# Gate tiles and turned q and k by two products, of 512 and of 256 columns, with their halves added by GpSimd, in place of three products of 256

## The reference, cut to what matters

```
# block 1
(q_a, k_a, v_a, f_a, q_b, k_b, v_b, q_c, c_kv, q_i, k_i, w_i, gates) = jnp.split(h @ w_in, ...)
...                                   # forgetting, stick-breaking and top-k attention
g_a, g_b, g_c = jnp.split(jax.nn.sigmoid(gates), N_BRANCH, axis=-1)
merged = (g_a * (y_a @ w_up_fox) + g_b * (y_b @ w_up_sb) + g_c * (y_c @ w_up_dsa))
return merged @ w_out
# block 2
q_a, k_a, v_a, q_b, k_b, v_b, gate_a, gate_b = jnp.split(h @ w_in, IN_OFFSETS, axis=-1)
...                                   # windowed attention and block attention
mixed = jax.nn.sigmoid(gate_a) * y_a + jax.nn.sigmoid(gate_b) * y_b
x = x + gt1[:, None, :] * (mixed @ w_out)
```

## Time and profile before

| | us |
|---|---|
| median of 3 runs | 2033.84 |
| lowest, highest | 2031.59, 2033.9 |
| the profiled execution | 2032.25 |
| its span | 2030.6 |
| PE busy in the span | 1960.0 (97%) |
| DVE busy | 1526.7 (75%) |
| ACT busy | 1031.0 (51%) |
| POOL busy | 44.9 (2%) |

### The profile page before, as it was taken

How to read it: one execution, slowest core, us unless ns; L and a number is a source line. 1 busy time by engine, 2 the same in 40 slices (tenths; PEclk the granted TensorE clock), 3 DMA queues, 4 the chain that set the end, 5 groups by cost and what they waited for, 6 DMA issues and landing times.

```text
span 2030.6 us, 32702 instructions
## 1 busy us (share of the span) xinstructions
PE 1960.0 (97%) x11980; PEld 1718.1 (85%) x11980; DVE 1526.7 (75%) x2637; ACT 1031.0 (51%) x1582; POOL 44.9 (2%) x80
## 2 busy tenths in 40 slices
PE   7999999999999999999899999999999999999998
PEld 6888898988888888899888888888788888887887
DVE  7887567579888987657678887785767778667766
ACT  5445545654446444545565445566444455555443
POOL 0000000000000000000000000000000000000000
PEclk9999999999999999999999999999999999999999
DMA  7874543257774876453246774441455544233553
GB/s 298 293 283 172 190 156 131 88 180 280 277 268 153 287 281 215 167 186 125 94 169 247 282 250 150 170 149 71 145 186 186 186 179 173 95 125 135 186 186 135
DMA packets 77286, 382.18 MB, mean 188 GB/s; under 512 B 9296, under 2 KB 9472, under 8 KB 55936
## 3 DMA queue, kind: packets, MB, share of 16 engines
q1 hardware_dynamic: 67392, 329.78, 44.9%
q0 software_dynamic: 9792, 51.00, 7.6%
HBM read 379.65 MB, written 1.10 MB: 188 GB/s over the span
## 4 chain that ended last, share of the span: by engine, by line
PE 82%; DVE 9%; ACT 6%; issue 3%; DMA 1%; SPq 0%; DVEq 0%; ACTq 0%
PE psum L674 21%; PE psum L585 15%; PE psum L586 15%; PE psum L587 15%; PE psum L677 11%; DVE weights_low_a L1446 2%; ACT weights_high_a L1069 1%; PE psum L883 1%; ACT x_normed L1077 1%; PE psum L821 1%; PE psum L812 1%; PE psum L910 1%; PE psum L911 1%; PE psum L909 1%; DMA raw_a<-in_w_ffn_a_a 1%
## 5 line engine op out<-in xcount | busy, mean ns | idle before, releaser
L674 PE MATMUL psum<-h_high_low,weights_high_a 128*128 128x512 f32 x1840 | 654.7, 398 | 5.4 <-DVE h_high_low L1491 3.3
L1446 DVE TENSOR_TENSOR weights_low_a<-raw_a,weights_high_a 128x2048 fp32r<-128x2048 f32 (+1 forms) x232 | 459.8, 1983 | 123.2 <-ACT weights_high_a L1069 121.2
L677 PE MATMUL psum<-h_high_low,weights_low_a 128*128 128x256 f32 x1840 | 514.2, 279 | 0.0
L674 PEld LDWEIGHTS psum<-h_high_low,weights_high_a 128*128 128x128 f32 x1840 | 345.3, 188 | 92.5 <-issue 5.3
L1069 ACT ACTIVATE weights_high_a<-raw_a 128x2048 fp32r<-128x2048 f32 (+1 forms) x232 | 386.0, 1664 | 65.1 <-PE psum L587 61.4
L677 PEld LDWEIGHTS psum<-h_high_low,weights_low_a 128*128 128x128 f32 x1840 | 346.7, 188 | 6.6 <-issue 1.0
L1446 DVE TENSOR_TENSOR weights_low_b<-raw_b,weights_high_b 128x1024 fp32r<-128x1024 f32 x224 | 273.3, 1220 | 54.5 <-ACT weights_high_b L1069 54.0
L1069 ACT ACTIVATE weights_high_b<-raw_b 128x1024 fp32r<-128x1024 f32 x224 | 235.4, 1052 | 104.6 <-PE psum L587 104.6
L1139 ACT ACTIVATE up_low_products<-psum 128x512 f32<-128x512 f32 (+1 forms) x146 | 74.1, 507 | 391.7 <-PE psum L677 391.6
L585 PE MATMUL psum<-weights_high_b,gated_high 128*128 128x512 f32 x608 | 241.8, 398 | 4.6 <-DVE gated_low L1575 2.8
L587 PE MATMUL psum<-weights_high_b,gated_low 128*128 128x512 f32 x608 | 241.3, 397 | 0.0
(11 more groups left out here) (300 smaller groups left out, 3165.9 us busy)
## 6 DMA issues: line engine op xcount, KB each, us to landing
ada_weights<-in_w_ada POOLq DMA_DIRECT2D x64, 768.0 KB, 5.9
raw_a<-in_w_ffn_a_a SPq DMA_DIRECT2D x44, 1024.0 KB, 7.3
raw_a<-in_w_ffn_b_a SPq DMA_DIRECT2D x44, 1024.0 KB, 7.4
raw_a<-in_w_ffn_a SPq DMA_DIRECT2D x64, 512.0 KB, 4.4
raw_b<-in_w_ffn_b SPq DMA_DIRECT2D x64, 512.0 KB, 3.3
raw_a<-in_w_proj_a SPq DMA_DIRECT2D x28, 1024.0 KB, 5.5
raw_a<-in_w_gate_a SPq DMA_DIRECT2D x26, 1024.0 KB, 4.8
raw_b<-in_w_ffn_a_b SPq DMA_DIRECT2D x44, 512.0 KB, 3.9
```

The source lines that it names most:

```text
L674: pe.matmul(ps[:, bank, :], whi[0][:, p, c:c + P], hboth[:, k, :, :].rearrange("p a b -> p (a b)"), start=k == 0, stop=False, skip_group_c ...
L677: last_mm = pe.matmul(ps[:, bank, SEQ:2 * SEQ], wlo[0][:, p, c:c + P], hhi[:, k, :], start=False, stop=k == KD - 1, skip_group_check=True)
L1446: dve.tensor_tensor(wlo[kind][:, p, 0:width], raw[kind][:, p, 0:width], whi[kind][:, p, 0:width].bitcast(F32), ALU.subtract).then_inc(lo_r ...
```

## The change

The two forms of product get one function, `mm2`. In each of the 832 steps, one matmul of 512 columns multiplies the high weights with `hhi` and `hlo`, and one of 256 columns adds the low weights by `hhi` to the second half. ACT copies the whole bank (512 columns) to SBUF, and GpSimd adds the second half onto the first. The second half of a copy lies where the first half of the next tile goes, so each copy waits until the add before it is done (`halves_added`). The q and k tiles and the gates of block 1 become one tensor for that, with a spare tile at its end. PE waits for the twelfth add before the first tick of block 1, and the turning of the gates waits for the adds instead of for the copies.

```
+            def mm2(both_halves, w_hi, w_lo, k, start, stop):
+
+                pe.matmul(both_halves, w_hi, hboth[:, k, :, :].rearrange("p a b -> p (a b)"), start=start, stop=False,
+                          skip_group_check=True)
+                return pe.matmul(both_halves[:, SEQ:2 * SEQ], w_lo, hhi[:, k, :], start=False, stop=stop,
+                                 skip_group_check=True)
...
@@ gate_tile (PE)
-                    m = mm3(ps[:, g % 2, 0:SEQ], hi, lo, hhi[:, k, :], hlo[:, k, :], k == 0, k == KD - 1)
+                    m = mm2(ps[:, g % 2, :], hi, lo, k, k == 0, k == KD - 1)
...
@@ project_turned (PE)
-                        m = mm3(ps[:, bank, 0:SEQ], whi[kind][:, n % 2, c:c + P], wlo[kind][:, n % 2, c:c + P],
-                                hhi[:, k, :], hlo[:, k, :], k == 0, k == KD - 1)
+                        m = mm2(ps[:, bank, :], whi[kind][:, n % 2, c:c + P], wlo[kind][:, n % 2, c:c + P],
+                                k, k == 0, k == KD - 1)
...
@@ ticks (PE)
                 pe.wait_ge(now().proj_copied, 20 if blk == 1 else 12)
+                if blk == 1:
+                    pe.wait_ge(now().halves_added, QK_TILES)
...
@@ GpSimd
+            def add_halves(tile, copied, value):
+
+                pool.wait_ge(copied, value)
+                pool.tensor_tensor(tile[:, 0, :], tile[:, 0, :], tile[:, 1, :], ALU.add).then_inc(now().halves_added, 1)
...
+                if blk == 2:
+                    for g in range(GATE2_TILES):
+                        add_halves(g2[:, g:g + 2, :], now().gate_copied, g + 1)
                 if blk == 1:
 
+                    for i in range(QK_TILES):
+                        add_halves(turned_and_gates[:, i:i + 2, :], now().proj_copied, 8 + i + 1)
+                    for g in range(GATE1_TILES):
+                        add_halves(g1[:, g:g + 2, :], now().gate_copied, g + 1)
                     pool.wait_ge(now().scale_ready, 2 * NT + 1)
                     ada_loads(l, 1)
...
@@ project_turned (ACT)
-                    copy_projection(w.mark[g], qk1[:, s, m, :], ps[:, (g + 8) % ROW_BANKS, 0:SEQ],
+                    if g:
+                        act.wait_ge(now().halves_added, g)
+                    copy_projection(w.mark[g], turned_and_gates[:, g:g + 2, :].rearrange("p a b -> p (a b)"),
+                                    ps[:, (g + 8) % ROW_BANKS, :],
                                     SCALE if s in (0, 2) else 1.0)
...
@@ gate_tile (ACT)
-                act.activation((g1 if blk == 1 else g2)[:, g, :], ps[:, g % 2, 0:SEQ],
+                added = g + (QK_TILES if blk == 1 else 0)
+                if added:
+                    act.wait_ge(now().halves_added, added)
+                act.activation((g1 if blk == 1 else g2)[:, g:g + 2, :].rearrange("p a b -> p (a b)"), ps[:, g % 2, :],
                                ACT.Copy).then_inc(now().gate_copied, 1)
...
@@ gate_tanh (ACT)
-                act.wait_ge(now().gate_copied, (f + 1) * n)
+                act.wait_ge(now().halves_added, (f + 1) * n + (QK_TILES if blk == 1 else 0))
```

More of the change, by code:

```diff
@@ L39 @@
 YT2 = 8
+QK_TILES, GATE1_TILES, GATE2_TILES = 12, 24, 16
 TA, TB = 16, 8
@@ L128, in __init__ @@
         self.gate_copied = one("gate_copied")
+        self.halves_added = one("halves_added")
         self.gates_ready = one("gates_ready")
@@ L349, in build @@
         tt2 = put("turned_two", [P, 14, SEQ])
-        g2 = put("gates_two", [P, 16, SEQ])
+        g2 = put("gates_two", [P, GATE2_TILES + 1, SEQ])
         y2 = put("y_two", [P, NT, YT2 * P])
```

5 lines of the change are left out of this document (3 added, 2 removed).

## The result

The median went from 2033.84 us to 2043.22 us (5 runs of each, 2037.06 to 2044.91 for the changed kernel). The ratio is 1.0042, with a 95% interval of 1.0031 to 1.0054: slower by 8.5 us, between 6 and 11. The forecast was 2030.5 us, and the result lies outside its range. The profiled execution of the changed kernel is the slowest of its five, 2044.91 us with a span of 2043.2.

The account below looks back on a forecast made before the run. PE was taken to bound the kernel, with 82% of the chain of waits. Products -7.2, copies +2.2 and passage +1.7 summed to -3.3 us: 2030.5 us, own range 2028 to 2033.5, over all rivals 2027.2 to 2039.5.

Parts of the forecast that it names:

- the gain of the products: Turned q and k and gates of both blocks: two matmuls a step in place of three, 7.2 us gained together.
- the passage: Turned projection to block 1's first tick: PE waits for the last add, 0.85 us longer, twice, 1.7 us.
- The step on PE: Turned and gate tiles: a step falls from 360 to 349.7 ns, 10.3 ns less, bounds 7.5 and 13.
- The weights by the chain's shares: Gates in the ticks: 74% of block 1's gain and 87% of block 2's count; turned tiles all on the path.
- The copies: ACT's copies of 512 columns: 0.22 us more each, 104 times; only those in the chain count, 2.2 us.
- The adds in the ticks: 104 GpSimd adds of 529 ns each, 55 us spread over 455 us; POOL never late, no cost in the ticks.
- rival (b): Passage and ticks: (a), and the clock falls too; 2039.5 to 2042.7, say 2041 us; chance 12%.
- (a): Passage and ticks: GpSimd and DVE hold each other up, +2.3 and +3.2 us, 2036.0 us in all; chance 30%.

Follow-up runs that it names:

- free adds of a tile to itself: The change without its own adds, plus 104 GpSimd adds of a spare tile to itself that nobody waits for; against the kernel before: 2033.62 us, 1.0005.
- free adds of two different rows: The change without its own adds, plus 104 GpSimd adds of two different constant rows, nobody waiting; against the kernel before: 2035.80 us, 1.0015.
- the spare rows: The change with PE's wait moved to the first scores and second halves copied to two spare rows in turn; against the kernel before: 2037.06 us, 1.0021.
- the fills: The kernel before plus 104 GpSimd memsets of 128x256, which write SBUF and read nothing, nobody waiting: 2033.75 us, 0.9999.
- the adds alone: The kernel before plus 104 GpSimd adds of a spare tile to itself, released by the same copies, nobody waiting: 2037.03 us, 1.0019.
- the late wait: The change with PE's wait for the twelfth add moved from before the first gate tile to the first scores reading q and k: 2038.76 us, 1.0022.

## Why the prediction was wrong

The runs form a ladder, in which each kernel has one thing more than the one above it. Each step is uncertain by about 2.6 us, the last by 3, so the four small ones don't stand clear of the noise by themselves; the two rows of free adds together (+4.2) and the last step do.

```
                                          ratio    step, us   forecast, us
products alone                            0.9987     -2.6       -7.2
+ copies of 512                           0.9994     +1.4       +2.2
+ free adds of a tile to itself           1.0005     +2.2     }   0
+ free adds of two different rows         1.0015     +2.0     }
+ copies, tanh, scores behind the adds    1.0022     +1.4         0
+ the wait before the first gate tile     1.0042     +4.1       +1.7
sum                                                  +8.5       -3.3
```

The sum is off by 11.8 us, at three steps: the gain of the products came out 4.6 us too small, adds that nobody waits for were put at nothing and take 4.2, and the passage takes 2.4 more than was put down.

- **The step on PE was nearly right.** "I take the middle, 349.7 ns: 10.3 ns less for a step." In the turned tiles it is 7.0 ns less, in the gate tiles some 9: 192 x 7.0 + 640 x 8.7 ns = 6.9 us on PE in place of 8.6.
- **The weights by the chain's shares are a failed step: they were too large.** I let 74% and 87% of the gates' gain through, and all of the turned tiles'. Of 6.9 us, 2.6 arrived (0.8 to 4.5), where these weights give 5.8. The chain says where the last wait ended with the lengths as they were. That DVE and ACT take over in places where they had been just behind, once PE's part is shorter, is my explanation, and no run isolates it; the clock's share is 1.9 us larger here than in the kernel before, which may be a part of it too.
- **The copies were right, as far as it can be told.** 0.60 us each, +1.4 against +2.2, with an uncertainty of 2.6. That they wait for adds, another 13.8 us of ACT's time in the trace, costs nothing that the spare rows could win back.
- **The adds in the ticks are the second failed step: put at nothing, they cost 3.9 us alone and 4.2 in the ladder.** The add was mis-sized, and its cost looked for in the wrong place. I took 529 ns, the length of a POOL instruction that issues a DMA, which says nothing of arithmetic. Undisturbed it is 0.73 us. More important, "POOL itself is never late" looked at POOL alone. The cost isn't that POOL is late, it is that DVE is held up: 17 us more for the same instructions. The clearest cases are small rotations that follow a split. How much of the 3.9 us is DVE late for PE and how much the lower clock isn't separated: 2.0 and 2.3 us in the one profile.
- **The passage is the third failed step**: "The copy is 0.22 us longer, the add takes 0.53 and its handover another 0.1: 0.85 us". It grew by 2.34 us, since the add ran beside a split and took 1.81. In the medians the wait there costs 4.1 us (7.0 by the profiles, with the fall of the clock behind it) where I had 1.7.

What the profile shows is rival (b): (a) and a fall of the clock as well, put at 2041 us with a chance of 12%. Its condition, "once PE stands still for some 3 us at the passage", was met with 2.87. That its time is so near is partly luck. It keeps the 7.2 us of the products, of which 2.6 came, and it puts 1.7 + 2.3 + 5 = 9 us at the passage and in the clock behind it, where the medians have 4.1; the two errors cancel. (a)'s picture had one detail wrong: the add doesn't start when the split ends. It starts when its copy ends, and is stretched until some 0.5 to 0.6 us after the split. It comes to the same end within 0.3 us (282.94 against the 283.25 that I had), which is why only the length of an add, and not its start, betrays the lock. The Trainium skill states such a lock in "SBUF — State Buffer", section "SBUF: two separate sides"; the fills that cost nothing (0.9999) and the adds that do (1.0019) agree with it. (a)'s number for the ticks, six places of 0.53 us, +3.2, was nearly right: the two rows of free adds have +4.2, and the trace of the adds alone has six places too, though one a layer in block 1 and two in block 2, of 0.2 to 0.4 us. The Trainium skill's "GPSIMD Engine Reference", section "Performance versus the Vector engine", gave 0.83 us as an estimate for the add by its ratio of 1.96; here it is 0.73 against 0.42, 1.74 times.

I had the right mechanism among the rivals and gave it 42% with (a), but I weighed it by DVE's idle share (76 of 112 us busy). In the ticks of the first layer GpSimd is now busy for 22.5 us and DVE for 74 of some 111. Two such engines meet often; most meetings cost nothing, and the idle time elsewhere doesn't undo the few that PE waits behind.

Open: how much of the 2.0 us between the two kinds of free add is their length, why so little of the products' gain arrives, and whether the fall at the passage costs what the profile shows, since the clock over all executions shows no more loss than in the late wait. Whether the two more falls in block 2's second layer belong to the change isn't settled either; the late wait has one there too, the kernel before has none in its profiled execution.

## What to carry to other kernels

Work given to GpSimd is not free because GpSimd is idle. If it reads SBUF, ask which VectorE instructions it will meet, and which of those the critical engine waits behind: here 104 adds that nobody waited for kept VectorE busy for 14.3 us more, and cost 3.9 us. The fills cost nothing.

A share of the chain is the most that a shorter operation can give, not what it will give. Here PE had 6.9 us less to do, the shares promised 5.8, and 2.6 came.

When a wait on a new engine lands at a point where PE has nothing else, look at what runs beside the new instruction there, not at its free length, and look whether the clock falls behind the hole. If the reader comes later, put the wait at the reader: this alone brought back 4.1 of 8.5 us (1 to 7 by the intervals).

## What the runs showed of the hardware

- A GpSimd add of 128x256 float32 takes 0.73 us with two different inputs and 0.61 with one tile as both; VectorE's takes 0.42. A fill takes 0.31.
- An add that begins more than 1 us before the end of a 2.29 us split of VectorE, which reads two SBUF tensors, takes 1.6 to 2.6 us. All 18 adds that begin inside such a split end 0.58 to 0.61 us behind it (0.47 with one tile as both inputs), and the rotation behind the split at the passage takes 0.76 or 0.65 us in place of 0.23.
- PE idle for 2.83 and 2.87 us before the gates: the granted clock went to 0.50 for 3.4 us. Idle for 0.80, or filled with small products for 2.96: it stayed at 1.00. The length of the hole alone doesn't tell: in block 2 of the change, holes of 1.44 and 1.54 us had a fall of 3.4 us behind them in the second layer and none in the first.
- One product of 512 columns and one of 256 take 353 ns in the turned projection, three of 256 take 360. In the gate tiles, with the first step of each, it is 361 and 370. A matmul and its load of weights less in each step are worth 7 to 9 ns.
